# Two small remainders, one behind the other: an order on VectorE in each expert's second step

## The chip, the cores and the metric

One core of a Trainium2 chip runs the kernel. The metric is the device time of one execution in microseconds (us); the time before is the median of three runs. Lower is better.

## What is computed

One sequence of 256 positions, width 1024, in fp32, passes a first block and then a second one. The first block has two layers: attention with a gated convolution and a dense SwiGLU, then a spatial gate and a mixture of experts. The second has two layers of four kinds of attention with a squared-ReLU MLP. The change lies in the mixture of experts, of which the reference says:

```python
D_FF = 2816
N_EXPERTS = 8
TOP_K = 2

def moe_swiglu(h, router_w, w1, w3, w2):
    """Top-2-of-8 expert SwiGLU; tokens sorted by expert into padded blocks, only selected
    experts evaluated. h: (B,S,D); w1,w3: (E,D,F); w2: (E,F,D)."""
    ...
    def expert_block(args):
        xb, e = args
        return (jax.nn.silu(xb @ w1[e]) * (xb @ w3[e])) @ w2[e]
    ...
    contrib = y_sorted * gate_flat[order][:, None].astype(h.dtype)
    out = jax.ops.segment_sum(contrib, sorted_token, num_segments=n_tok)
```

## The kernel before

**Products in three parts.** Each operand of a large product is held as a high part `hi` in fp32r, a rounded form, and a remainder `lo` = value - `hi`. `product` (lines 519 to 521) issues three matmuls: hi x hi, then the two mixed ones. So each weight passes two engines before TensorE may use it. ScalarE copies a half slot (128 x 1024) from the ring into a buffer `w_hi` (line 2147), and VectorE subtracts it from the ring's value into `w_lo` (line 1312). The same is done to hidden features (`h_hi`, line 2410, and `h_lo`, line 1900) and to the outputs of an expert (`y_hi`, line 2416, and `y_lo`, line 1914).

**The stream of weights.** SyncE streams slots of 1 MB from HBM into a ring of six buffers (line 491). The refill of a buffer waits for `lo_ready` of both halves that it held, so for VectorE. The `w_hi`/`w_lo` buffers of the expert stage are four; the copy of half m waits until TensorE has done half m - 4. `reach(done)` says how many halves can be split once TensorE has done `done` of them, and `split_to(m)` splits all halves before m.

**The expert stage.** Eight experts of 11 steps each make 88 steps `s`, with `e = s // 11` and `j = s % 11`. A step takes three slots, six halves: four halves for the up products of 256 hidden features (w1 and w3 side by side), two for the down product of the step before. TensorE's order in a step is: two up halves, the transposes of the step before (`moe_turn`), two further up halves, the down product `moe_down(s - 1)`. The down product waits for `lo_ready` of its first half and for `moe.hidT_lo`, which `moe_lo(s - 1)` raises on VectorE; in the first down product of an expert also for `y_split`, since it starts to overwrite the banks from which `y_lo` is made.

**VectorE's order.** `moe_step` (lines 1918 to 1936) writes it out. It is `split_to`, `moe_lo(s - 1)` (the tile `h_lo`), `split_to` for two further halves, and the product of silu and gate (line 1929, written to a part of `arena`). In steps 2 and 3 of an expert the outputs of the expert before are merged (line 1906), one half of the tokens each. In the second step (j = 1) of experts 2 to 8 the remainder of the expert outputs is made too, by `split_y`: two instructions of 128 x 512. All engines run their queues in order, and a wait holds what stands behind it.

**ScalarE's order** in that second step is: `y_hi`, `w_hi` of both down halves, `h_hi`, then the next `w_hi`.

Of the kernel before, what the change touches and what calls it, by code (L numbers as in the profile page):

```python
# [108 lines left out]
def ada_before(n):  # L109

    q = PLACE["work", n]
    out = []
    while q and ORDER[q - 1][0] == "ada":
        q -= 1
        out.insert(0, ORDER[q][1])
    return out
# [16 lines left out]
def reach(done):  # L133

    m = done
    while m < 2 * SLOTS and BEFORE[m] < done:
        m += 1
    return m
# [5 lines left out]
def up_slot(s):  # L144

    return W_MOE + (3 * s - 1 if s else 0)
# [71 lines left out]
def build(nc, a, out):  # L218
# [3 lines left out]
    with ExitStack() as ctx:  # L222
# [101 lines left out]
        def half_buffer(m):  # L324
            b = BUFFER[m]
            return (w_hi[:, b, :], w_lo[:, b, :]) if b < PAIRS else (w_hi3[:, :], w_lo3[:, :])
# [944 lines left out]
        def _(dve):  # L1271
# [10 lines left out]
            def fold(slot):  # L1282

                l, q = slot // ADA_SLOTS, PLACE["ada", slot]
                dve.wait_ge(landed[q % RING], 16 * (q // RING + 1))
                for h in range(2):
                    i = 2 * (slot % ADA_SLOTS) + h
                    k, part = i // 6, i % 6
                    src = ring[:, q % RING, h * HALF:(h + 1) * HALF]
                    c = csilu[:, k:k + 1]  # L1290
                    if k == 0 and part < 4:
                        ins = dve.tensor_scalar(acc[:, part, :], src, c, None, ALU.mult)
                    else:
                        if k == 0:
                            dve.wait_ge(bada_in, 16 * (l + 1))
                        else:
                            dve.wait_ge(folded, 2 * ADA_SLOTS * l + i - 5)
                        ins = dve.scalar_tensor_tensor(out=acc[:, part, :], in0=src, scalar=c, in1=acc[:, part, :],  # L1298
                                                       op0=ALU.mult, op1=ALU.add)
                    ins.then_inc(folded, 1)  # L1300

            def split_to(m_end):

                for m in range(split_at[0], min(m_end, split_end[0])):
                    if m % 2 == 0:
                        for slot in ada_before(m // 2):
                            fold(slot)
                    dve.wait_ge(hi_ready, m + 1)
                    a = m % 2 * HALF
                    hi, lo = half_buffer(m)  # L1310
                    q = PLACE["work", m // 2]
                    dve.tensor_tensor(lo, ring[:, q % RING, a:a + HALF], hi.bitcast(F32), ALU.subtract)\  # L1312
                        .then_inc(lo_ready, 1)
                    split_at[0] = m + 1
# [562 lines left out]
            def select(w, n):  # L1877

                rank = col("slot", w.chunk * P, P)
                e = slice(n, n + 1) if isinstance(n, int) else bass.ds(n, 1)  # L1880
                for t in range(QB):
                    pl = place[:, t, e]
                    ins = dve.tensor_scalar(sel[:, t, :], rank, pl, None, ALU.is_equal)
                    if w is second_pass:
                        ins = dve.tensor_scalar(selg[:, t, :], rank, pl, gate[:, t, e], ALU.is_equal, ALU.mult)
                ins.then_inc(w.sel_ready, 1)

            def take(w, counts, c0=0):

                for h in range(2):  # L1890
                    dve.wait_ge(w.gathered_hi, counts[h])
                    f = slice(4 * h, 4 * h + 4)
                    dve.tensor_tensor(x_lo[:, f, c0:c0 + P], ps[:, 6 + h, :].rearrange("p (f c) -> p f c", f=4), x_hi[:, f, c0:c0 + P].bitcast(F32),
                                      ALU.subtract).then_inc(w.gathered_lo, 1)

            def moe_lo(s):

                dve.wait_ge(moe.hidT_hi, s + 1)
                c = 256 * (s % 2)
                dve.tensor_tensor(h_lo[:, s % 2, 0:256], ps[:, 2, c:c + 256], h_hi[:, s % 2, 0:256].bitcast(F32),  # L1900
                                  ALU.subtract).then_inc(moe.hidT_lo, 1)

            def moe_merge(e, t):

                dve.wait_ge(moe.scattered, 2 * e + t + 1)
                dve.scalar_tensor_tensor(out=resid[:, t, :], in0=bank(merge_bank(e, t), 2), scalar=gate[:, t, e:e + 1],  # L1906
                                         in1=resid[:, t, :], op0=ALU.mult, op1=ALU.add).then_inc(moe.merged, 1)

            def split_y(e):

                for h in range(2):
                    c = slice(h * BANK, (h + 1) * BANK)
                    dve.wait_ge(moe.y_kept, 2 * e + h + 1)
                    dve.tensor_tensor(y_lo[:, c], ps[:, 4 + h, :], y_hi[:, c].bitcast(F32), ALU.subtract)\
                        .then_inc(y_split, 1)

            def moe_step(s):

                e, j = s // J1, s % J1
                n = up_slot(s)  # L1920
                if s >= 1:
                    if j == 1 and e >= 1:
                        split_to(reach(2 * n + 1))
                        split_y(e - 1)
                    split_to(reach(2 * (n + 1)))
                    moe_lo(s - 1)
                split_to(reach(2 * (n + 2)))
                dve.wait_ge(moe.act_ready, s + 1)
                dve.tensor_tensor(hid_rows[:, s % 2, :], act_rows[:, s % 2, :], ps[:, s % 2, 256:512], ALU.mult)                    .then_inc(moe.hid_ready, 1)
                if e >= 1 and j in (2, 3):  # L1930
                    moe_merge(e - 1, j - 2)
                if j == 6 and e + 1 < NE:
                    dve.wait_ge(moe.selT_ready, e + 1)
                    select(moe, e + 1)
                if j == 8 and e + 1 < NE:
                    take(moe, [2 * e + 3, 2 * e + 4], P * ((e + 1) % 2))
# [52 lines left out]
            for s in range(STEPS):  # L1989
                moe_step(s)  # L1990
# [831 lines left out]
```

## Time and profile before

| | us |
|---|---|
| median of 3 runs | 2073.05 |
| lowest and highest of them | 2065.96, 2076.78 |
| the profiled execution | 2076.95 |
| its span, first to last instruction | 2074.8 |
| TensorE busy (PE) | 1970.3 |
| VectorE busy (DVE) | 1591.0 |
| ScalarE busy (ACT) | 1192.3 |

The profile is of one execution, which is not one of the three. Its busy times are shares of the span; what an engine waits for stands in the idle time ahead of an instruction. PE is TensorE's matmuls, PEld its weight loads, which overlap them. The expert stage lies between about 485 and 1287 us.

### The profile page before, as it was taken

To read this page: it belongs to the slowest core of one execution; us is meant where nothing else is said; L and a number is where in the kernel's file an instruction comes from. 1 tells how busy PE (TensorE), PEld (TensorE's weight loads), DVE (VectorE), ACT (ScalarE), POOL (GpSimd) and SP (SyncE) were. 2 spreads that over 40 slices of the span, in tenths; PEclk is the share of its full clock that TensorE was granted. 3 is DMA by queue.
4 is the path that set the end of the run, shared out by engine and by line. 5 is a ranking of instruction groups with operands and counts; after the bars stand their busy time and mean duration, and the time that the engine had idled before them with its cause. 6 is when DMAs were issued, how large, how long until landed. Compare 5 with 4: busy or idle time off the path is not lost.

```text
span 2074.8 us, 27900 instructions
## 1 busy us (share of the span) xinstructions
PE 1970.3 (95%) x11086; PEld 1694.4 (82%) x11086; DVE 1591.0 (77%) x1997; ACT 1192.3 (57%) x1638; POOL 29.8 (1%) x32
## 2 busy tenths in 40 slices
PE   7999999999999999999999998897999999899998
PEld 7889997877878787878787876797789988778997
DVE  5868886658898989898989897767479984746555
ACT  4444345337777777777777775556444445534443
POOL 0000000000000000000000000000000000000000
PEclk9999999999999999999999999899999999889999
DMA  7349885437888989898888887342168862304551
GB/s 298 138 143 348 330 331 188 173 112 296 340 340 342 344 339 343 338 341 342 339 342 338 343 343 293 122 142 102 61 234 344 337 257 107 122 28 166 183 188 56
DMA packets 71405, 512.02 MB, mean 247 GB/s; under 512 B 8162, under 2 KB 8546, under 8 KB 9826
## 3 DMA queue, kind: packets, MB, share of 16 engines
q1 hardware_dynamic: 69536, 504.40, 64.5%
q10 hardware_dynamic: 1732, 5.77, 0.8%
q8 instruction: 90, 1.47, 0.3%
q14 instruction: 47, 0.39, 0.1%
HBM read 509.08 MB, written 1.05 MB: 246 GB/s over the span
## 4 chain that ended last, share of the span: by engine, by line
PE 80%; DVE 12%; ACT 4%; issue 2%; POOL 1%; DMA 0%; POOLq 0%; ACTq 0%; SPq 0%; DVEq 0%
PE ps L519 24%; PE ps L521 23%; PE ps L520 23%; DVE w_lo L1312 6%; ACT w_hi L2147 2%; PE ps L732 1%; PE ps L945 1%; PE ps L528 1%; PE ps L684 1%; PE ps L698 1%; POOL stat L2592 1%; PE ps L963 1%; PE ps L790 1%; ACT score L2255 1%; DVE resid L1906 0%
## 5 line engine op out<-in xcount | busy, mean ns | idle before, releaser
L1312 DVE TENSOR_TENSOR w_lo<-ring,w_hi 128x1024 fp32r<-128x1024 f32 x862 | 1044.6, 1222 | 331.4 <-ACT w_hi L2147 304.0
L2147 ACT ACTIVATE w_hi<-ring 128x1024 fp32r<-128x1024 f32 x862 | 911.5, 1061 | 662.8 <-PE ps L521 655.9
L519 PE MATMUL ps<-w_hi,x_hi 128*128 128x512 f32 (+1 forms) x1056 | 408.5, 389 | 7.2 <-DVE x_lo L1600 3.3
L521 PE MATMUL ps<-w_hi,x_lo 128*128 128x512 f32 (+1 forms) x1056 | 400.4, 381 | 0.0
L520 PE MATMUL ps<-w_lo,x_hi 128*128 128x512 f32 (+1 forms) x1056 | 399.4, 380 | 0.0
L519 PE MATMUL ps<-x_hi,w_hi 128*128 128x256 f32 x1248 | 359.5, 288 | 5.0 <-DVE x_lo L1426 3.9
L520 PE MATMUL ps<-x_lo,w_hi 128*128 128x256 f32 x1248 | 355.1, 285 | 0.0
L521 PE MATMUL ps<-x_hi,w_lo 128*128 128x256 f32 x1248 | 354.8, 284 | 0.0
L519 PE MATMUL ps<-w_hi,h_hi 128*128 128x512 f32 x732 | 291.9, 399 | 18.7 <-DVE h_lo L1900 15.7
L520 PE MATMUL ps<-w_lo,h_hi 128*128 128x512 f32 x732 | 285.6, 390 | 0.0
L521 PE MATMUL ps<-w_hi,h_lo 128*128 128x512 f32 x732 | 285.1, 390 | 0.0
L519 PEld LDWEIGHTS ps<-x_hi,w_hi 128*128 128x128 f32 x1248 | 241.4, 193 | 10.6 <-issue 5.1
L520 PEld LDWEIGHTS ps<-x_lo,w_hi 128*128 128x128 f32 x1248 | 241.5, 194 | 1.7 <-issue 0.2
L521 PEld LDWEIGHTS ps<-x_hi,w_lo 128*128 128x128 f32 x1248 | 241.3, 193 | 0.0
L519 PEld LDWEIGHTS ps<-w_hi,x_hi 128*128 128x128 f32 (+1 forms) x1056 | 193.1, 183 | 48.1 <-DVE w_lo L1312 4.0
L521 PEld LDWEIGHTS ps<-w_hi,x_lo 128*128 128x128 f32 (+1 forms) x1056 | 192.7, 183 | 40.5
L520 PEld LDWEIGHTS ps<-w_lo,x_hi 128*128 128x128 f32 (+1 forms) x1056 | 193.3, 183 | 36.6
L519 PEld LDWEIGHTS ps<-w_hi,h_hi 128*128 128x128 f32 x732 | 137.7, 188 | 63.2 <-DVE h_lo L1900 34.4
L521 PEld LDWEIGHTS ps<-w_hi,h_lo 128*128 128x128 f32 x732 | 137.7, 188 | 29.6
L520 PEld LDWEIGHTS ps<-w_lo,h_hi 128*128 128x128 f32 x732 | 138.0, 188 | 25.0
L1298 DVE SCALAR_TENSOR_TENSOR arena<-ring,csilu,arena 128x1024 f32<-128x1024 f32 x88 | 108.9, 1278 | 0.0
L2255 ACT ACTIVATE score<-score,soft 128x128 f32<-128x128 f32 (+4 forms) x112 | 47.2, 424 | 34.7 <-DVE soft L1498 34.6
(269 smaller groups left out, 1459.0 us busy)
## 6 DMA issues: line engine op xcount, KB each, us to landing
ring<-in_stream SPq DMA_DIRECT2D x479, 1024.0 KB, 4.9
con<-in_consts ACTq DMA_DIRECT2D x1, 2048.0 KB, 21.7
arena<-in_ln_rows ACTq DMA_DIRECT2D x3, 512.0 KB, 3.9
resid<-in_x SPq DMA_DIRECT2D x1, 1024.0 KB, 6.6
arena<-in_fin_row ACTq DMA_DIRECT2D x2, 512.0 KB, 3.4
out<-rows SPq DMA_DIRECT2D x2, 512.0 KB, 2.6
arena<-in_w_s ACTq DMA_DIRECT2D x1, 512.0 KB, 5.9
con<-in_consts ACTq DMA_DIRECT2D x1, 237.0 KB, 4.3
```

What stands on the lines that cost most here:

```text
L519: pe.matmul(out_, lhs[0], rhs[0], start=start, stop=False)
L520: pe.matmul(out_, lhs[0], rhs[1], start=False, stop=False)
L521: return pe.matmul(out_, lhs[1], rhs[0], start=False, stop=stop)
L528: pe.matmul(ps[:, b, :], x_hi[:, 6, 0:P], x_lo[:, 4:6, :].rearrange("p a s -> p (a s)"), start=True, stop=True)
L684: last = pe.matmul(ps[:, b + u // 2, (u % 2) * S:(u % 2) * S + kw], q, k, start=True, stop=True)
L698: last = pe.transpose(ps[0:kp, 4 + n // 4, (n % 4) * P:(n % 4 + 1) * P], score[:, g % 2, u, kb * P:kb * P + kp], ident)
L732: last = pe.matmul(ps[:, mix_bank(layer, g), o * vw:(o + 1) * vw], probT[0:kp, g % 2, u * nkb + kb, :], v, start=kb == 0, stop=kb == nkb - 1)
L790: last = pe.matmul(ps[:, COLUMN_BANK[l][p0 // 2], c:c + 1], acc[:, part, f * P:(f + 1) * P], ones[:, 0:1], start=True, stop=True)
L1298: ins = dve.scalar_tensor_tensor(out=acc[:, part, :], in0=src, scalar=c, in1=acc[:, part, :], op0=ALU.mult, op1=ALU.add)
L1312: dve.tensor_tensor(lo, ring[:, q % RING, a:a + HALF], hi.bitcast(F32), ALU.subtract)\
L2147: act.activation(half_buffer(m)[0], ring[:, q % RING, a:a + HALF], ACT.Copy).then_inc(hi_ready, 1)
L2255: ins = act.activation(sc, sc, ACT.Exp, bias=soft[:, g % 4, 0, u:u + 1], scale=96.0 ** -0.5 if kind == "mla" else 0.125, accum_out=soft[:, ...
```

## The change

In the steps that make `y_lo` (j = 1 and e >= 1, seven of the 88), `moe_lo(s - 1)` is issued directly behind `split_y`, and the `split_to` that stood ahead of it comes after it. In the other steps the order is kept, in an `else` branch. Since `split_to(reach(2 * n + 1))` has already been issued in such a step, the `split_to` that is moved covers one half: the second half of the down slot.

```diff
                     if j == 1 and e >= 1:
                         split_to(reach(2 * n + 1))
                         split_y(e - 1)
-                    split_to(reach(2 * (n + 1)))
-                    moe_lo(s - 1)
+                        moe_lo(s - 1)
+                        split_to(reach(2 * (n + 1)))
+                    else:
+                        split_to(reach(2 * (n + 1)))
+                        moe_lo(s - 1)
                 split_to(reach(2 * (n + 2)))
```

VectorE's queue before, in the second step of the second expert, with what each instruction waits for:

```order
L1312 TENSOR_TENSOR w_lo<-ring,w_hi 128x1024 [waits hi_ready] x3
L1914 TENSOR_TENSOR y_lo<-ps,y_hi 128x512 [waits moe_y_kept] x2
L1312 TENSOR_TENSOR w_lo_51<-ring,w_hi_50 128x1024 [waits hi_ready]
L1900 TENSOR_TENSOR h_lo<-ps,h_hi 128x256 [waits moe_hidT_hi]
L1312 TENSOR_TENSOR w_lo<-ring,w_hi 128x1024 [waits hi_ready] x2
L1929 TENSOR_TENSOR arena<-arena,ps 128x256 [waits moe_act_ready]
```

The same place with the change (`w_lo_51` and `w_hi_50` are the fourth pair of weight buffers):

```order
L1312 TENSOR_TENSOR w_lo<-ring,w_hi 128x1024 [waits hi_ready] x3
L1914 TENSOR_TENSOR y_lo<-ps,y_hi 128x512 [waits moe_y_kept] x2
L1900 TENSOR_TENSOR h_lo<-ps,h_hi 128x256 [waits moe_hidT_hi]
L1312 TENSOR_TENSOR w_lo_51<-ring,w_hi_50 128x1024 [waits hi_ready]
L1312 TENSOR_TENSOR w_lo<-ring,w_hi 128x1024 [waits hi_ready] x2
L1932 TENSOR_TENSOR arena<-arena,ps 128x256 [waits moe_act_ready]
```

`h_lo` and the remainder of the down slot's second half have changed places; line 1929 is now called 1932.

TensorE's queue at the down product of the same step, which is the same in both kernels:

```order
L521 MATMUL ps<-w_hi,x_lo 128x512
L519 MATMUL ps<-w_hi,h_hi 128x512 [waits lo_ready,y_split,moe_hidT_lo]
L520 MATMUL ps<-w_lo,h_hi 128x512
L521 MATMUL ps<-w_hi,h_lo 128x512
L519 MATMUL ps<-w_hi,h_hi 128x512
L520 MATMUL ps<-w_lo,h_hi 128x512
L521 MATMUL ps<-w_hi,h_lo 128x512
L519 MATMUL ps<-w_hi_50,h_hi 128x512 [waits lo_ready]
```

Nothing moved here: the first of the six waits for `h_lo` and the first half's remainder, and the second half's remainder is asked for six matmuls later.

## Rows read from the trace of the kernel before

**Rows 1.** The page: busy time, granted TensorE clock in 40 slices, chain by engine.

```profile
PE 1970.3 (95%) x11086; PEld 1694.4 (82%) x11086; DVE 1591.0 (77%) x1997; ACT 1192.3 (57%) x1638; POOL 29.8 (1%) x32
...
PEclk9999999999999999999999999899999999889999
...
PE 80%; DVE 12%; ACT 4%; issue 2%; POOL 1%; DMA 0%; POOLq 0%; ACTq 0%; SPq 0%; DVEq 0%
```

**Rows 2.** Line 1900: who waited for `h_lo`, with us in all and times.

```profile
  PEld ps L519: 34.4, 59
  PE ps L519: 15.7, 22
```

**Rows 3.** TensorE in order of time: start, duration, instruction, idle time before it, releaser.

```profile
559.84 0.50 PE L519 MATMUL ps<-w_hi,h_hi 128*128 128x512 f32 x1 [0.31 <-DVE h_lo L1900]
...
587.02 0.50 PE L519 MATMUL ps<-w_hi,h_hi 128*128 128x512 f32 x1 [1.36 <-DVE h_lo L1900]
...
614.90 0.50 PE L519 MATMUL ps<-w_hi,h_hi 128*128 128x512 f32 x1 [0.43 <-DVE h_lo L1900]
...
688.87 0.50 PE L519 MATMUL ps<-w_hi,h_hi 128*128 128x512 f32 x1 [1.34 <-DVE h_lo L1900]
...
1198.37 0.50 PE L519 MATMUL ps<-w_hi,h_hi 128*128 128x512 f32 x1 [1.34 <-DVE h_lo L1900]
```

**Rows 4.** VectorE in order of time, steps 2 and 3 of the second expert.

```profile
583.08 1.22 DVE L1312 TENSOR_TENSOR w_lo<-ring,w_hi 128x1024 fp32r<-128x1024 f32 x1 [0.69 <-ACT w_hi L2147]
584.22 1.28 DVE L1914 TENSOR_TENSOR y_lo<-ps,y_hi 128x512 fp32r<-128x512 f32 x2
585.42 1.21 DVE L1312 TENSOR_TENSOR w_lo<-ring,w_hi 128x1024 fp32r<-128x1024 f32 x1
586.55 0.41 DVE L1900 TENSOR_TENSOR h_lo<-ps,h_hi 128x256 fp32r<-128x256 f32 x1
586.88 2.35 DVE L1312 TENSOR_TENSOR w_lo<-ring,w_hi 128x1024 fp32r<-128x1024 f32 x2
589.15 0.41 DVE L1929 TENSOR_TENSOR arena<-arena,ps 128x256 f32<-128x256 f32 x1
589.88 1.23 DVE L1312 TENSOR_TENSOR w_lo<-ring,w_hi 128x1024 fp32r<-128x1024 f32 x1 [0.32 <-ACT w_hi L2147]
591.26 3.95 DVE L1312 TENSOR_TENSOR w_lo<-ring,w_hi 128x1024 fp32r<-128x1024 f32 x3 [0.16 <-ACT w_hi L2147]
595.13 0.42 DVE L1900 TENSOR_TENSOR h_lo<-ps,h_hi 128x256 fp32r<-128x256 f32 x1
596.52 2.59 DVE L1312 TENSOR_TENSOR w_lo<-ring,w_hi 128x1024 fp32r<-128x1024 f32 x2 [0.98 <-ACT w_hi L2147]
599.03 0.41 DVE L1929 TENSOR_TENSOR arena<-arena,ps 128x256 f32<-128x256 f32 x1
599.36 1.28 DVE L1906 SCALAR_TENSOR_TENSOR resid<-ps,gate,resid 128x1024 f32<-128x1024 f32 x1
```

**Rows 5.** ScalarE in order of time, second step of the second expert.

```profile
583.88 0.38 ACT L2410 ACTIVATE h_hi<-ps 128x256 fp32r<-128x256 f32 x1
...
588.79 1.06 ACT L2147 ACTIVATE w_hi<-ring 128x1024 fp32r<-128x1024 f32 x1 [1.70 <-PE ps L521]
```

**Rows 6.** TensorE in order of time, its down product there and in the next step.

```profile
585.27 0.39 PE L521 MATMUL ps<-w_hi,x_lo 128*128 128x512 f32 x1
...
588.53 0.39 PE L519 MATMUL ps<-w_hi,h_hi 128*128 128x512 f32 x1
...
596.53 0.39 PE L519 MATMUL ps<-w_hi,h_hi 128*128 128x512 f32 x1
```

**Rows 7.** Line 491, us to landing; who kept ScalarE's line 2147 idle.

```profile
DMA to landing us min/median/max: 4.6/4.9/25.3
...
  DMA ring<-in_stream: 2.1, 1
```

**Rows 8.** Busy us by engine in stretches, then granted clock, DMA share, GB/s.

```profile
598.70:607.70 9.00, 9.00 (x43) 7.38 (x42) 8.51 (x10) 6.57 (x9) 0.00 (x0) 1.00 0.79 289
...
500.00:1280.00 780.00, 765.13 (x3520) 620.73 (x3519) 699.51 (x735) 597.01 (x715) 0.00 (x0) 1.00 0.90 342
1290.00:2074.00 784.00, 724.29 (x4628) 644.33 (x4627) 528.01 (x773) 366.36 (x609) 13.13 (x13) 0.95 0.44 162
```

## The prediction

> **What bounds the kernel now.** I read the page first: its busy shares, the granted clock by slice and the engine shares of the chain that ended last [rows 1]. TensorE is busy for 95% of the span and holds 80% of the chain, VectorE 12%. So a change on VectorE is worth only what TensorE waits for it. Next I read what waits for the feature remainder `h_lo` (line 1900): in the whole run TensorE's matmuls stood idle 15.7 us for it, in 22 waits [rows 2]. That is the ceiling of anything done for `h_lo`. Then TensorE's own order of time shows where those waits are [rows 3]. They repeat with each expert: about 1.35 us in the second step (j = 1), 0.43 us in the fifth (j = 4), about 0.3 us in the tenth (j = 9). The seven of the second step (experts 2 to 8; 1.36 once, 1.34 the other six times) make 1.36 + 6 x 1.34 = 9.4 us. The change touches these seven alone.
>
> Last I read VectorE, ScalarE and TensorE side by side around one of the seven, the second expert's at 587 us [rows 4, 5, 6]. TensorE has started its last up matmul at 585.27 (0.39 long, so done at 585.66) and needs `h_lo` for the down product. VectorE does meanwhile: weight remainder of the down slot's first half at 583.08, two `y_lo` from 584.22, weight remainder of the second half at 585.42, `h_lo` at 586.55. ScalarE's `h_hi`, from which `h_lo` is made, had been ready since 583.88 + 0.38 = 584.26. `h_lo` therefore waits for nothing but its place in VectorE's queue; it ends at 586.55 + 0.41 = 586.96, and TensorE starts at 587.02, 0.06 later.
>
> **The change, part by part.** Nothing is added or removed, no DMA is moved on its queue, and TensorE and ScalarE keep their orders. On VectorE, in seven places, `h_lo` changes places with one 128x1024 weight remainder.
>
> (a) *`h_lo` comes earlier.* VectorE's slot after the two `y_lo` opens at 585.42. There `h_lo` starts instead of at 586.55: 1.13 us earlier, one weight remainder from start to start (its own duration is 1.21, neighbours overlap by 0.08) [rows 4]. It ends at 585.42 + 0.41 = 585.83, and TensorE can start at 585.89 instead of 587.02. Its last matmul ended at 585.66, so it is still `h_lo` that is awaited, 0.23 us long. Gain: 1.13 us each, 7 x 1.13 = 7.9 us. The other six show the same wait to 0.02 us [rows 3], so I take them alike.
> The Trainium skill, Advanced Engine Details, section The Read-Write Bubble, says that the memory latency of VectorE lies open between instructions, the bus being pipelined within a tile but not between two. Taken strictly, the instruction moved away would be worth its whole 1.21 us and the seven 8.5 us; the rows with their overlap of 0.08 say 1.13, and the sum goes by the rows.
>
> (b) *The second half's remainder comes later.* It starts 0.33 us (586.88 - 586.55, the step from an `h_lo` to the next start) behind 585.42, at 585.75, and ends at 586.96 instead of 585.42 + 1.21 = 586.63. Who waits for it? TensorE's seventh matmul of the down product, which comes 588.53 - 587.02 = 1.51 us behind the first [rows 6]: now at 585.89 + 1.51 = 587.40. The remainder is there 0.44 us before. So it costs nothing; if the cover were gone, its price would be the part of its 1.21 us that sticks out. The refill of the ring's buffer also waits for this remainder and goes out 0.33 us later. SyncE's issues take 4.9 us (median) to land, in the whole run ScalarE waited once, 2.1 us, for a landing [rows 7], while a ring of six slots lies ahead. I cost it at nothing; as the rival on the refills it could be 7 x 0.33 = 2.3 us.
>
> (c) *The new wait.* `h_lo` waits for `h_hi`, and the second half's remainder, two more remainders and the product of line 1929 now stand behind that wait. `h_hi` is ready at 584.26, 1.16 us before 585.42 [rows 4, 5]: no cost. If it were later, the gain would fall one for one with what it is past 585.42, and be gone at 1.13 us.
>
> (d) *Is the gain kept?* From 586.88 on VectorE does the same work at the same times as before, while TensorE is 1.13 us ahead: VectorE is the one that is late. The test is whether it gets back its old distance before TensorE needs it. TensorE's down product of the first half ends earlier, so ScalarE's next weight copy, which waits for it, starts at 588.79 - 1.13 = 587.66 and is done at 588.72 [rows 5]. VectorE, after the line 1929 product at 589.15, is free for the next start at 589.15 + 0.33 = 589.48 (0.33 as from 599.03 to 599.36; before, it stood idle until 589.88). Four remainders at 1.13 each bring it to 594.0, and it then starts the `h_lo` of the next step, before at 595.13: 1.1 us earlier. The idle time before those four and inside them, 0.32, 0.16 and the gap inside the 3.95 us of three (3.95 against 1.21 + 2 x 1.13 = 3.47: 0.48), makes 0.96 and with the overlaps lost at each restart about 1.1 [rows 4]. Even if it lacked a tenth, 0.98 us of idle time stand directly behind that `h_lo` [rows 4], and TensorE wants that `h_lo` only at 596.53 - 1.13 = 595.40 [rows 6], with it done at 594.0 + 0.42 = 594.4. So by the end of the third step (j = 2) all three engines stand as before, 1.13 us earlier, and the waits of the fifth and tenth step stay at 0.43 and 0.3.
>
> **Sum.** 7 x 1.13 = 7.9 us off, with bounds of 7 x 1.13 - 2.3 = 5.6 (the refills of (b) on the path) and 9.4 (each of the seven waits gone). The profiled execution took 2076.95 us, 3.9 above the median of the three runs (2073.05); from it 2069.0, from the median 2073.05 - 7.9 = 2065.1. I give the one for the median. It is 0.38%. About 0.5% (10.4 us) is what a measurement of this kernel can tell from no change, and the three runs themselves lie 10.8 us apart, so I expect a true gain that counts as no change.
>
> **The rivals.**
> *The gain is taken back later (no change, 2073.0).* VectorE would be the bound of steps j = 2 to 4: it is busy for 8.51 of 9.00 us in one stretch there [rows 8], and it has a merge of 1.28 us in each of two steps. Then the wait of the fifth step would grow from 0.43 to 0.43 + 1.13 = 1.56. Against it stands the idle time of 0.98 us before 596.52, ended by ScalarE, which itself waits for TensorE: VectorE has caught up by then. It would decide only if the catching up of (d) fell short by over 2 us.
> *The refills become the path (slower, 2075.4).* The place is the ring buffer that is free only when the second half's remainder is done, 0.33 us later than before. The stage streams at a DMA share of 0.90 [rows 8], so there is little rate to spare; if ScalarE's copies waited for landings, each expert would lose the 0.33 and TensorE, waiting for weights, would have no use for the early `h_lo`: 2073.05 + 7 x 0.33 = 2075.4. It decides from the point at which a landing comes after ScalarE asks for it. One expert takes 688.87 - 587.02 = 101.85 us [rows 3] for 33 slots, 3.09 each; a buffer is wanted again about five slots after its refill goes out, 15 us, and the landing takes 4.9. So it is some 10 us from that point.
> *The clock falls elsewhere (about 2055 or 2075).* In the expert stage the granted clock is 1.00, i.e. 2.4 GHz, in spite of waits of 1.3 us; from 1290 us on it is 0.95 [rows 8], which is about a tenth of 784 us at the lower level, 78 us, costing half of them, 39. That stage gets the same work at other instants. A quarter more or less of it would be 10 us: 2065.1 - 10 = 2055, 2065.1 + 10 = 2075.
> The Trainium skill, TensorE: Matmul & The Clock Gate, Part 1, says that the instant at which the clock changes varies from run to run of one kernel. By that rule neither sign is favoured, and the 10.8 us between three runs of one kernel speak for it.
>
> **How the numbers follow.** Forecast (7.9 us off, waits of the second step down to 0.23): 0.74. Taken back later: 0.09. Refills on the path: 0.03. Clock elsewhere: 0.14, half of it each way. Predicted time: 2065.1. The forecast with its bounds and the uncertainty of a median of such runs (3 to 4 us) spans 2060 to 2070; the other cases are let in up to 2057.5 below and 2073.5 above, which takes in "taken back", leaves out both clock ends and the refills, and some of the scatter. Faster by over 0.5% needs 10.4 us: the scatter of the medians lifts 7.9 over it in about a fifth of the forecast's cases (0.15), plus the clock's good half (0.07): 0.22. Slower by over 0.5%: 0.02, the refills or the clock's bad half with scatter on top. Within 0.5%: the rest, 0.76.
>
> **What would show it.** In the profile after, TensorE's waits for `h_lo` fall from 15.7 to about 15.7 - 7.9 = 7.8 us, still 22 of them, the seven at 0.2 to 0.25. `h_lo` starts about 1.2 us behind the first `y_lo`, the second half's remainder 0.33 behind `h_lo`, and no wait for `w_lo` appears at the seventh down matmul. The distance between second steps of neighbouring experts (101.85 us) shrinks to 100.7. The fifth step's wait stays at 0.43. I am wrong if that one grows, if TensorE waits for line 1312, if ScalarE waits for landings in the expert stage, or if the expert stage is 8 us shorter and the rest after it longer.

## The result

| | before | with the change |
|---|---|---|
| median of 19 runs each, us | 2074.51 | 2063.65 |
| lowest and highest, us | 2065.96, 2080.97 | 2058.24, 2070.19 |
| profiled execution, us (span) | 2076.95 (2074.8) | 2059.92 (2057.8) |
| ratio, 95% interval | | 0.9943, 0.993 to 0.9955 |

The change makes the kernel faster by 0.57% by the ratio, with an interval of 0.45 to 0.70%. The medians lie 10.9 us (0.52%) apart, against the 7.9 us of the forecast. The profile after separates the two parts of this at once: the expert stage got shorter by nearly what was predicted, and the rest comes from elsewhere.

Line 1900 first, who waited for `h_lo`, in the kernel after (it answers [rows 2]):

```profile
  PEld ps L519: 26.5, 59
  PE ps L519: 7.8, 22
```

TensorE's matmuls wait 7.8 us where it was 15.7, in the same 22 places. TensorE in order of time, kernel after (start, duration, instruction, idle before it; it answers [rows 3, 6]):

```profile
585.30 0.39 PE L521 MATMUL ps<-w_hi,x_lo 128*128 128x512 f32 x1
585.89 0.50 PE L519 MATMUL ps<-w_hi,h_hi 128*128 128x512 f32 x1 [0.21 <-DVE h_lo L1900]
586.23 0.39 PE L520 MATMUL ps<-w_lo,h_hi 128*128 128x512 f32 x1
...
613.74 0.51 PE L519 MATMUL ps<-w_hi,h_hi 128*128 128x512 f32 x1 [0.44 <-DVE h_lo L1900]
...
686.62 0.50 PE L519 MATMUL ps<-w_hi,h_hi 128*128 128x512 f32 x1 [0.20 <-DVE h_lo L1900]
```

The wait of the second step has gone from 1.36 to 0.21 us, that of the fifth stays (0.44 against 0.43), and from one second step to the next it is 686.62 - 585.89 = 100.73 us instead of 101.85. VectorE in order of time, kernel after (it answers [rows 4]):

```profile
584.22 1.28 DVE L1914 TENSOR_TENSOR y_lo<-ps,y_hi 128x512 fp32r<-128x512 f32 x2
585.42 0.42 DVE L1900 TENSOR_TENSOR h_lo<-ps,h_hi 128x256 fp32r<-128x256 f32 x1
585.75 3.49 DVE L1312 TENSOR_TENSOR w_lo<-ring,w_hi 128x1024 fp32r<-128x1024 f32 x3
589.16 0.42 DVE L1932 TENSOR_TENSOR arena<-arena,ps 128x256 f32<-128x256 f32 x1
589.49 4.63 DVE L1312 TENSOR_TENSOR w_lo<-ring,w_hi 128x1024 fp32r<-128x1024 f32 x4
594.03 0.42 DVE L1900 TENSOR_TENSOR h_lo<-ps,h_hi 128x256 fp32r<-128x256 f32 x1
595.36 2.59 DVE L1312 TENSOR_TENSOR w_lo<-ring,w_hi 128x1024 fp32r<-128x1024 f32 x2 [0.92 <-ACT w_hi L2150]
```

`h_lo` starts at 585.42, the second half's remainder 0.33 behind it. From 589.49 VectorE does four remainders without a pause, where it had paused before each of the first two; by the next `h_lo` (594.03, before 595.13) it has caught up, and the pause behind it is 0.92 us (before 0.98). The length of the expert stage is taken from the start of its first transposes (line 963) to the start of the last expert's scatter (line 992). In the kernel before:

```profile
484.18 0.33 PE L963 MATMUL ps<-con,arena 128*128 128x128 f32 x1 [0.64 <-DVE arena L1929]
...
1287.07 0.74 PE L992 MATMUL ps<-y_hi,h_hi 128*128 128x512 f32 x1 [2.06 <-issue]
```

and after:

```profile
484.19 0.33 PE L963 MATMUL ps<-con,arena 128*128 128x128 f32 x1 [0.65 <-DVE arena L1932]
...
1279.33 0.47 PE L992 MATMUL ps<-y_hi,h_hi 128*128 128x512 f32 x1 [2.06 <-issue]
```

802.89 us have become 795.14: 7.75 less. The stage begins at the same time. What follows it took 2074.8 - 1287.07 = 787.7 us before and 2057.8 - 1279.33 = 778.5 after, 9.2 less, though none of its code was changed and TensorE has the same 4634 matmuls there in both traces. The same stretch of time by granted clock, before and then after (columns: busy us of PE, PEld, DVE, ACT, POOL, granted clock, DMA share, GB/s; it answers the last line of [rows 8]):

```profile
1290.00:2050.00 760.00, 708.56 (x4542) 630.84 (x4542) 513.75 (x756) 359.98 (x599) 11.65 (x11) 0.95 0.45 166
```

```profile
1290.00:2050.00 760.00, 715.45 (x4624) 637.67 (x4622) 519.64 (x757) 361.75 (x599) 10.58 (x10) 0.96 0.45 166
```

The work of after stands 7.75 us earlier in this stretch; in the 760 us TensorE issued 82 matmuls more, at a higher mean clock. This one pair of executions is an extreme one; how much of it stands in the medians is the second question of the experiments.

### The profile page after: what moved, and what is told of

The parts are those of the page before. It is cut to its first block, busy times and chain, and to the rows that moved or that the text cites. A ratio compares the mean times of both kernels' runs of the same rounds, so it can differ in the third digit from the quotient of the medians.

```text
span 2057.8 us, 27900 instructions
## 1 busy us (share of the span) xinstructions
PE 1962.3 (95%) x11086; PEld 1689.2 (82%) x11086; DVE 1589.1 (77%) x1997; ACT 1192.9 (58%) x1638; POOL 29.9 (1%) x32
## 4 chain that ended last, share of the span: by engine, by line
PE 80%; DVE 12%; ACT 4%; issue 2%; POOL 1%; DMA 0%; POOLq 0%; ACTq 0%; DVEq 0%
PE ps L519 24%; PE ps L521 23%; PE ps L520 23%; DVE w_lo L1312 6%; ACT w_hi L2150 2%; PE ps L945 1%; PE ps L732 1%; PE ps L528 1%; PE ps L684 1%; PE ps L698 1%; POOL stat L2595 1%; PE ps L963 1%; ACT score L2258 1%; PE ps L790 1%; PE ps L536 1%
## 5 line engine op out<-in xcount | busy, mean ns | idle before, releaser
L519 PE MATMUL ps<-w_hi,h_hi 128*128 128x512 f32 x732 | 292.5, 400 | 10.8 <-DVE h_lo L1900 7.8
```

The source lines that it names most:

```text
L519: pe.matmul(out_, lhs[0], rhs[0], start=start, stop=False)
```

## The experiments

Two questions were asked: whether the place of `h_lo` in the queue is the whole of the 7.75 us, and what the 3 us beyond are. "Stage" below is the expert stage as just measured, in each kernel's own profile, and "sum of waits" is what TensorE's matmuls stood idle for `h_lo`. A ratio is the time against that of the kernel before measured beside it, with its 95% interval. The edits show the lines that matter; where nothing else is said they are made in the kernel with the change.

### 1. One place further back

Against the kernel before, in the seven second steps alone:

```diff
                         split_y(e - 1)
-                    split_to(reach(2 * (n + 1)))
-                    moe_lo(s - 1)
+                        split_to(reach(2 * (n + 1)) + 1)
+                        moe_lo(s - 1)
```

> The opposite dose: in the seven second steps h_lo stands one weight remainder further back than before, behind the first half of the next slot too. Theory (h_lo's place in VectorE's queue is the whole wait, 1.13 us a place, and the seven experts are alike): TensorE's seven waits grow from 1.34 to about 2.47 us, its sum of waits for h_lo from 15.7 to 23.6, the expert stage is 7.9 us longer than before, the waits of the fifth step stay at 0.43. Rival (VectorE's load in steps j = 2 to 4 is the bound): part of the delay is absorbed or carried on, the fifth step's wait moves away from 0.43. For the whole time: 7.9 us slower than before (ratio 1.0038) if the extra gain of the change over 7.9 us was chance in the clock; more than that, about 12 (1.0057), if the shift itself moves the clock in a lasting way.

The sum of waits is 23.5 us, and the seven waits are 2.49 and six times 2.47. So the waits grew as expected. The stage, though, is 815.5 us, 12.6 more than before and not 7.9. The rest is the clock. TensorE in order of time in this kernel, second and fourth expert:

```profile
587.70 0.79 PE L519 MATMUL ps<-w_hi,h_hi 128*128 128x512 f32 x1 [2.49 <-DVE h_lo L1900]
588.29 0.63 PE L520 MATMUL ps<-w_lo,h_hi 128*128 128x512 f32 x1
588.72 0.63 PE L521 MATMUL ps<-w_hi,h_lo 128*128 128x512 f32 x1
...
796.70 0.50 PE L519 MATMUL ps<-w_hi,h_hi 128*128 128x512 f32 x1 [2.47 <-DVE h_lo L1900]
797.03 0.40 PE L520 MATMUL ps<-w_lo,h_hi 128*128 128x512 f32 x1
797.27 0.39 PE L521 MATMUL ps<-w_hi,h_lo 128*128 128x512 f32 x1
```

Behind one wait the matmuls take 0.63 us and follow one another by 0.43, behind an equal one 0.39 and 0.24. The busy time by stretch says why (clock is the third number from the right):

```profile
587.70:591.10 3.40, 3.40 (x8) 2.72 (x9) 1.41 (x2) 0.37 (x1) 0.00 (x0) 0.52 0.92 364
692.10:695.50 3.40, 3.37 (x10) 2.70 (x11) 1.72 (x3) 1.06 (x1) 0.00 (x0) 0.69 0.95 364
1002.90:1006.30 3.40, 3.37 (x10) 2.70 (x11) 1.57 (x3) 1.06 (x1) 0.00 (x0) 0.66 0.94 361
796.70:800.10 3.40, 3.40 (x15) 2.83 (x16) 1.97 (x3) 1.35 (x2) 0.00 (x0) 1.00 0.95 378
```

Behind three of the seven waits of 2.5 us the granted clock fell to the lower level, 1.2 GHz, for a while; in the first of these stretches 8 matmuls were started where the undisturbed one has 15, so about 7 x 0.23 = 1.6 us were lost. Three times that is 4.8, and 7.9 + 4.8 = 12.7. The distances from one second step to the next bear it out: 104.4 to 104.6 us behind the three waits with the lower clock, 103.0 to 103.3 behind the others. Why three of seven equal waits had it and four had not, no run shows. Waits of 1.36 us and less did this nowhere in the stage, in any of the profiles. The whole time is 2086.79 us, ratio 1.0047 (1.003 to 1.0063), compatible with both of the numbers expected.

### 2. Four of the seven places

```diff
-                    if j == 1 and e >= 1:
+                    if j == 1 and e % 2 == 1:
                         split_to(reach(2 * n + 1))
                         split_y(e - 1)
                         moe_lo(s - 1)
                         split_to(reach(2 * (n + 1)))
```

(With even `e`, experts 3, 5 and 7, the order of before is kept.)

> The change in four of the seven places only (experts 2, 4, 6, 8). Theory: four waits of 0.20 and three of 1.34, sum of waits for h_lo 15.7 - 4 x 1.13 = 11.2 us, expert stage 4.5 us shorter than before. Whole time 4.5 us shorter (ratio 0.9978) if nothing but the expert stage counts; a share of four sevenths of the measured 0.57% (0.9967) if each saved microsecond brings more than itself.

Sum of waits 11.0 us, stage 798.5 us, 4.4 shorter than before: the saving goes by the place, one by one. The whole time gives 0.9966 (0.9953 to 0.998), which holds both expectations and is nearer to the second. In both experiments the waits of the fifth step stayed at 0.43 to 0.44, so nothing is left of the idea that VectorE's load in the following steps takes part of the gain.

### 3. The remainder of the expert outputs first

```diff
                     if j == 1 and e >= 1:
-                        split_to(reach(2 * n + 1))
+                        split_to(reach(2 * n))
                         split_y(e - 1)
+                        split_to(reach(2 * n + 1))
                         moe_lo(s - 1)
```

> The change, and y_lo is put ahead of the remainder of the down slot's first half, into the 0.69 us in which VectorE stood idle there. Theory: y_lo from about 582.4, first half's remainder about 583.5 to 584.7, h_lo at about 584.6, done at 585.0 before TensorE's last up matmul ends at 585.66; the seven waits of 0.20 go to zero, 1.4 us less than with the change alone, sum of waits for h_lo 7.8 - 1.4 = 6.4 us. Rival: the first half's remainder now comes last and TensorE waits for it (line 1312) instead, or y_lo waits for y_hi and the remainders behind it come late, so that the stage gets longer.

VectorE in order of time in this kernel, then TensorE:

```profile
580.77 1.28 DVE L1914 TENSOR_TENSOR y_lo<-ps,y_hi 128x512 fp32r<-128x512 f32 x2
581.97 1.22 DVE L1312 TENSOR_TENSOR w_lo<-ring,w_hi 128x1024 fp32r<-128x1024 f32 x1
583.10 0.42 DVE L1900 TENSOR_TENSOR h_lo<-ps,h_hi 128x256 fp32r<-128x256 f32 x1
```

```profile
583.76 0.39 PE L521 MATMUL ps<-w_hi,x_lo 128*128 128x512 f32 x1
583.98 0.39 PE L519 MATMUL ps<-w_hi,h_hi 128*128 128x512 f32 x1
584.21 0.39 PE L520 MATMUL ps<-w_lo,h_hi 128*128 128x512 f32 x1
```

VectorE's pause of 0.69 us has been filled, and the down product follows the up product with no gap. The waits fell as expected, to 6.4 us in 15 places. The stage fell by more: 791.35 us, 3.8 less than with the change alone, not 1.4. The reason is in the rows. With a wait, however small, the last matmul before it is booked with its whole 0.39 us, though the next could start 0.23 after it (583.98 to 584.21); and the first matmul after a wait takes 0.50 instead of 0.39 and lets the second start after 0.34 (585.89 to 586.23 in the kernel with the change) instead of 0.23. So a wait that goes away whole gives back its length and 0.16 + 0.11 = 0.27 us: 7 x (0.20 + 0.27) = 3.3 of the 3.8; for the other 0.5 there is no account. Whole time: 2063.13 us, ratio 0.9942 (0.9928 to 0.9956).

### 4. The fifth and the tenth step too

```diff
+                    elif j == 9 or (j == 4 and e >= 1):
+                        split_to(reach(2 * n + 1))
+                        moe_lo(s - 1)
+                        split_to(reach(2 * (n + 1)))
                     else:
```

> The change, and h_lo stands ahead of the down slot's second half in the fifth step (j = 4, experts 2 to 8) and in the tenth (j = 9, all) as well. Theory: their waits of 0.44 and 0.34 go to zero, 7 x 0.44 + 7 x 0.34 = 5.5 us off the expert stage against the change alone, and of TensorE's 22 waits for h_lo in the matmuls the seven of 0.20 and the last one of 0.93 stay: sum about 2.4 us. Rival (VectorE's load is the bound there, since the steps before hold the merges and x_lo): the waits come back a step later or at line 1312, and the stage keeps its length.

The sum of waits is 2.4 us, as expected, with eight places left, and none of the rival's waits for weight remainders came up. The stage is 785.5 us, 9.6 less than with the change alone, where 5.5 were expected; 14 removed waits with 0.27 each are 3.8 more, 9.3 together. Whole time: 2053.47 us, ratio 0.99 (0.9885 to 0.9915).

### 5. The same swap where there is no wait

Here the seven second steps have the order of before, and `elif j in (3, 6, 8)` has the three lines of experiment 4.

> Control: the order of before in the seven second steps, and the same swap (h_lo ahead of the down slot's second half) in the fourth, seventh and ninth steps of all experts, 24 places in which TensorE does not wait for h_lo. Theory: the swap is worth only the wait that it shortens, so nothing: 22 waits and 15.7 us as before, expert stage 802.9 us, ratio 1.000. Rival: the swap in itself does something (VectorE's overlaps, earlier or later refills of the ring), 24 x 0.05 us or more, or a wait for line 1312 opens since the second half's remainder comes later.

The whole time says "nothing" (0.999, 0.9972 to 1.0007), but the stage is 801.6 us, 1.3 less than before, and that is no noise: the same stage repeats to 0.1 us elsewhere (795.14 and 795.04 in experiment 7). The expectation was wrong in that "no matmul waits" is not "nothing waits". Line 1900 in this kernel:

```profile
  PEld ps L519: 31.1, 42
  PE ps L519: 16.6, 22
```

The weight loads' waits for `h_lo` went from 59 to 42. Such a place in the kernel before, TensorE's matmuls and weight loads in order of time:

```profile
504.31 0.39 PE L521 MATMUL ps<-w_hi,x_lo 128*128 128x512 f32 x1
504.51 0.19 PEld L519 LDWEIGHTS ps<-w_hi,h_hi 128*128 128x128 f32 x1 [0.24 <-DVE h_lo L1900]
504.53 0.48 PE L519 MATMUL ps<-w_hi,h_hi 128*128 128x512 f32 x1
504.62 0.19 PEld L520 LDWEIGHTS ps<-w_lo,h_hi 128*128 128x128 f32 x1
504.85 0.39 PE L520 MATMUL ps<-w_lo,h_hi 128*128 128x512 f32 x1
```

No idle time stands before the matmul, but its weights were loaded only with it, and the next one starts 0.32 us later instead of 0.23. In the same place of the control kernel the load stands one matmul ahead:

```profile
502.78 0.39 PE L521 MATMUL ps<-w_hi,x_lo 128*128 128x512 f32 x1
502.78 0.19 PEld L519 LDWEIGHTS ps<-w_hi,h_hi 128*128 128x128 f32 x1
503.00 0.39 PE L519 MATMUL ps<-w_hi,h_hi 128*128 128x512 f32 x1
...
503.23 0.39 PE L520 MATMUL ps<-w_lo,h_hi 128*128 128x512 f32 x1
```

17 places at about 0.1 us are 1.7 us; the waits of the tenth step grew by 0.13 on the average, 0.9 us in all (15.7 to 16.6), presumably since a remainder now comes later in the step before. The balance, 0.8, is a part of the 1.3 measured, not all of it.

### 6. Where the other 3 us are

Each run comes with its span and its mean granted clock. The clock has two levels, 2.4 GHz (1.0) and 1.2 GHz (0.5), so time at the lower level is 2 x (1 - clock) x span. Within the runs of one kernel, 196 over all the kernels, the span goes up by 0.37 us for each us of it. The table takes that out:

| kernel | runs | mean span | mean clock | us at the lower level | span less 0.37 of it | against before | stage against before |
|---|---|---|---|---|---|---|---|
| before | 70 | 2072.6 | 0.9744 | 106.0 | 2033.3 | | |
| change | 19 | 2061.5 | 0.9765 | 97.0 | 2025.7 | -7.6 | -7.8 |
| 1, further back | 7 | 2082.3 | 0.9740 | 108.3 | 2042.3 | +9.0 | +12.6 |
| 2, four of seven | 8 | 2065.5 | 0.9759 | 99.7 | 2028.6 | -4.7 | -4.4 |
| 3, y_lo first | 6 | 2060.0 | 0.9748 | 103.7 | 2021.6 | -11.7 | -11.5 |
| 4, three steps | 5 | 2050.9 | 0.9768 | 95.2 | 2015.7 | -17.6 | -17.4 |
| 5, swap without wait | 11 | 2069.9 | 0.9752 | 102.8 | 2031.9 | -1.4 | -1.3 |

At an equal clock each of these kernels gains what its expert stage gains, to 0.2 us (experiment 1, whose stage has clock losses of its own, apart). For the kernels of experiments 7 to 9 the same reckoning gives -8.0 for the change once more (stage -7.9), -6.0, -4.5, -1.1 and +0.7 with 8, 15, 25 and 34 matmuls added (stage -6.1, -4.3, -2.0 and +0.1), +0.1 for experiment 8 (stage +0.3) and -22.2 for experiment 9 (stage -21.1); so it holds to about 1 us. What the change has beyond 7.8 us is a clock of 0.9765 against 0.9744: 9.0 us less at the lower level, 0.37 x 9.0 = 3.3 us.

The clock records in the two profiles say where that time is. Ahead of the stage both have 23.9 us at the lower level, inside it none; behind it the kernel before has 88.0 and the change 62.5. These 25.5 us less, at 0.37, are 9.4 us, and the part behind the stage was 9.2 us shorter. But the profile of the same changed kernel in experiment 7 has 70.1 us there, so a single pair of executions proves nothing about the means.

Two reasons for the better mean clock were tried: that the later stages run at other instants, and that idle TensorE in the seven places lowers the clock elsewhere.

### 7. The change once more, and its later stages moved back

The first run is the change itself, beside the two that follow it.

> The change as it stands, once more, on the chip and at the time of the two that follow. Its waits must be those of the profile after (seven of 0.20, sum 7.8 us, expert stage 7.75 us shorter). Both theories on the remaining 3 to 4 us start from here: if the whole time is again 11 to 12 us below before, with a mean granted clock about 0.002 higher, the extra is lasting; if it is 7 to 8 us and the clocks are alike, the extra was chance.

Measured: 2064.35 us, ratio 0.9944 (0.9923 to 0.9965), sum of waits 7.8, stage 795.0, clock 0.9762. The 11 us are there again.

Then 34 matmuls of no use were put in a place where nothing waits for them (`keep_warm(n, 3)` issues n matmuls of 512 columns whose result nobody reads):

```diff
+                if e == NE - 1 and j == 8:
+                    keep_warm(34, 3)
                 for h in range(2):
                     moe_up(2 * n + h, 2 * h, s, c0)
```

> The change, and 34 matmuls of no use in the ninth step of the last expert, 34 x 0.227 = 7.7 us, so that all that follows the expert stage stands at the instants of the kernel before. Position theory (the stages behind the experts get a better clock because they begin 8 us earlier): clock and whole time go back to those of before, ratio 1.000. Other theory (what is saved is saved where it stood, and the clock is either chance or hangs on the seven waits): the change plus 7.7 us, so ratio to before about 0.9943 + 0.0037 = 0.998, clock as with the change.

The stage is 803.0 us long, as before the change; the seven waits are at 0.20. The whole time is 2074.37 us, ratio 0.9999 (0.9986 to 1.0011), clock 0.9748. The 0.998 of the other theory lies outside. The 7.9 us of padding cost 10 us between the medians.

> The change and 8 matmuls of no use in the ninth step of the last expert, 1.8 us. Nothing but the 1.8 us: 2064.0 + 1.8 = 2065.8, ratio to before 0.9952. Position theory (34 of them brought 10.9 instead of 7.7 us): the extra 3 us come in part or whole, at 0.4 us a microsecond 2066.5, or all at once 2069.

> The same with 15 matmuls, 3.4 us. Nothing but that: 2067.4, ratio 0.9960. Position theory: 2068.8 if gradual (ratio 0.9967), up to 2070.6 if all at once; or the time of the change plus 3.4 with its clock of 0.9765 if only the place within one stretch of the clock counts.

> The same with 25 matmuls, 5.7 us. Nothing but that: 2069.7, ratio 0.9972. Position theory: 2072 (ratio 0.9983), clock near 0.975.

| matmuls added | stage longer by | whole time, ratio (interval) | clock | mean span longer by |
|---|---|---|---|---|
| 8 | 1.7 | 2068.81, 0.9965 (0.9948 to 0.9981) | 0.9755 | 3.3 |
| 15 | 3.5 | 2068.13, 0.9965 (0.995 to 0.9981) | 0.9760 | 4.0 |
| 25 | 5.7 | 2074.89, 1.0 (0.9982 to 1.0017) | 0.9744 | 9.9 |
| 34 | 7.9 | 2074.37, 0.9999 (0.9986 to 1.0011) | 0.9748 | 11.1 |

The waits are those of the change in all four. With 1.7 and 3.5 us the time moves by little more than is added; with 5.7 and 7.9 the whole extra gain is gone. For the 25 matmuls "nothing but that" (0.9972) lies outside the interval. Whether it comes back gradually or all at once can't be told from these four. Nor did any run add the 25 or 34 matmuls to the kernel before, so that they lower the clock by themselves, and not by moving what follows, is not ruled out.

### 8. The waits filled with matmuls of no use

```diff
+                if e >= 1 and j == 1:
+                    keep_warm(5, 3)
                 if s >= 1:
                     moe_down(s - 1)
```

(in the kernel before)

> The order of before, and five matmuls of no use ahead of the down product in each of the seven second steps, 1.14 us, inside the 1.34 us in which TensorE waits for h_lo. No time is saved there: h_lo comes when it came, the seven waits shrink to about 0.2 us in name only, and the expert stage keeps its 802.9 us. Waits theory (idle TensorE in the seven places lowers the granted clock elsewhere or later): the clock rises to that of the change and 3 to 4 us of the time go. Other theory: time and clock of before, ratio 1.000 within 0.1 to 0.2%.

The seven waits are 0.21, the stage is 803.2 us, and the whole time is 2072.88 us, ratio 0.9991 (0.9978 to 1.0004), clock 0.9756. The interval holds both theories, so this run doesn't separate them. Its clock is 0.0012 (95% interval 0.0001 to 0.0023) above that of before, with the later stages at nearly the same instants; so a part of the 3 us may hang on the idle times. Against its being the whole stands experiment 7, where all four kernels have the change's short waits and two of them have lost the extra gain.

### 9. Both additions

> Both additions together: y_lo ahead of the first half's remainder in the second step, and h_lo ahead of the second half's remainder in the fifth and tenth. Theory: only the last wait for h_lo (0.93 us, end of the last expert) stays. A wait that goes away whole gives back its length and 0.27 us more (the end of a matmul's 0.39 us counts as busy though the next could start after 0.23, and the first one after a wait takes 0.11 longer): against the version with three steps 7 x (0.20 + 0.27) = 3.3 us off the expert stage, 785.5 - 3.3 = 782.2 us; whole time 20 to 24 us below before (ratio 0.990 to 0.988). Rival: the two additions share VectorE's idle time and one of them does not pay.

```diff
                     if j == 1 and e >= 1:
-                        split_to(reach(2 * n + 1))
+                        split_to(reach(2 * n))
                         split_y(e - 1)
+                        split_to(reach(2 * n + 1))
                         moe_lo(s - 1)
                         split_to(reach(2 * (n + 1)))
+                    elif j == 9 or (j == 4 and e >= 1):
+                        split_to(reach(2 * n + 1))
+                        moe_lo(s - 1)
+                        split_to(reach(2 * (n + 1)))
```

Line 1900 in this kernel:

```profile
  PEld ps L519: 10.4, 37
  PE ps L519: 0.9, 1
```

One wait in the matmuls is left. The stage is 781.8 us (expected 782.2), 21.1 less than before. Four runs have a median of 2049.46 us, ratio 0.9869 (0.9844 to 0.9893). This version beats both kernels. With the rule of 0.27 us a wait, learnt from experiments 3 and 4, the sum was right to half a us.

## Why the prediction came out as it did

**(a), the price of one place.** Right: `h_lo` at 585.42 and TensorE at 585.89, both to the hundredth, the seven waits at 0.20 to 0.21 where 0.2 to 0.25 were expected, the stage 7.75 us shorter against 7.9. Experiments 1 and 2 give the same price in the waits, with the opposite sign and in part. Here both ends of the comparison were waits that did not vanish; only so did the idle time shown give the saving. Two general statements ahead of (a) are wrong. The 15.7 us of waits are not "the ceiling of anything done for `h_lo`": experiment 9 took away 14.8 us of them and shortened the stage by 21.1, and experiment 3, with all seven waits gone, by 11.5, more than the bound of 9.4. And a change on VectorE is not worth "only what TensorE waits for it": experiment 5 gave 1.3 us with no less idle time in the matmuls, in part since weight loads were held up less. VectorE's instructions kept their start-to-start times, so the overlap of 0.08 us was rightly taken off. By the reading of the Trainium skill, Advanced Engine Details, section The Read-Write Bubble, at its strictest, a place is worth 1.21 us and the seven 8.5; the trace has `h_lo` 586.55 - 585.42 = 1.13 us earlier, so the measurement decides against it.

**(b), the second half's remainder.** Costed at nothing, and nothing came: it ran from 585.75, and in the whole run TensorE's matmuls waited 1.2 us for line 1312, where it was 1.8. The refills, 0.33 us later, were the rival with the price of 2.3 us; ScalarE still waited for a landing only once, 2.3 us (before 2.1), and the stage is no longer for it.

**(c), the new wait**, cost nothing. `h_hi` stood ready at 584.27, 1.15 us ahead of `h_lo`'s start.

**(d), whether VectorE catches up.** Right. The start times 589.48 and 594.0 and the wait of 0.43 in the fifth step were predicted; 589.49, 594.03 and 0.44 were measured. The rival "taken back later" falls with it.

**The sum is where the prediction was off**: 7.9 us against 10.9 between the medians. The measured time lies in the range, 1.5 us below the time forecast. That it is so near is in part luck: the median of three runs from which I started was 1.5 us below that of 19, which made up for half of the missing 3 us. The change came out at 0.52 to 0.57%, just beyond the 0.5% that I had taken as the border, to which I had given a chance of 0.22; the interval reaches down to 0.45%. The step that was off is the rival on the clock. It had the right place (all that stands behind 1290 us, at 0.95), and perhaps the right cause (the same work at other instants), but I took it as a coin with two equal sides, out of the sum. The runs show a difference that repeats: in 19 and again in 6 runs the change had 0.0018 to 0.0021 more of the clock (all 25 together 0.0020, 95% interval 0.0009 to 0.0030), worth 3 us, and in the kernel with 34 matmuls, which put the later stages back to their old instants, it was gone. I also charged half a us for each us at the lower level, where the runs show 0.37: the 78 us cost about 29 and not 39. The sign of the difference could not have been had from the trace of the kernel before. Its size could in part: the three runs, 10.8 us apart, and the 78 us at the lower level say that a few us of clock must be counted beside any saving of this size. The Trainium skill, TensorE: Matmul & The Clock Gate, Part 1, was read too broadly. It says that the instant of a change of clock varies from run to run of one kernel. That agrees with the traces: of two profiled executions of the changed kernel, one has a clock of 1.00 in its first 100 us, the other 0.98. That the means of two kernels should then be equal was my step, not the page's, and the runs contradict it.

**What stays open.** Why the mean clock of the changed kernel is better. That the later stages begin 7.8 us earlier is the likeliest reason by experiment 7, but it is not a rule of the kind "earlier is better". In experiment 3 they begin 11.5 us earlier and the clock is 0.9748, hardly that of before, in 4 and 9 17.4 and 21.1 us earlier with 0.9768 and 0.9760, and in 8 at the old instants with 0.9756. Each of these means, of 4 to 12 runs, is uncertain by 0.001 to 0.003. The steps of experiment 7 are too coarse for a law, and the profile is of one run of each kernel.

## What to carry to other kernels

Where a consumer waits for a small result that stands ready-to-make behind larger work in another engine's queue, moving it ahead is worth the number of places times the start-to-start distance there, as long as a wait is left, and that can be taken from one timeline; check only that what is put behind has a consumer that comes late enough. A wait that is shortened gives back what is shown, one that is removed gives back about 0.27 us more here, so the last 0.2 us of a wait are worth 0.47 or a little more. Ask for the mean clock of every run before a difference of a few tenths of a per cent is explained by the code: at an equal clock the kernels here agreed with their own traces to about 1 us (experiment 1 aside, which lost clock in the stage itself), without it they were off by up to 4 (experiment 4: mean span 21.7 us shorter, stage 17.4).

## What the runs showed of the hardware that was not expected

- Idle time before a matmul understates the wait. The matmul before it counts 0.39 us as busy where 0.23 would do, and the first one after it delays its successor by 0.11.
- A weight load that waited 0.24 us (504.51) cost 0.1 us though no matmul shows any idle time.
- With TensorE otherwise busy throughout, waits of up to 1.36 us never lowered the granted clock in the expert stage, and behind waits of 2.47 to 2.49 us it fell in three cases of seven, each costing about 1.6 us more.
- The mean granted clock differs between kernels whose later stages are the same code: 0.9765 and 0.9762 for the change, 0.9744 and 0.9748 with 25 and 34 matmuls added ahead of those stages. The span follows with 0.37 us for each us at the lower level. What sets the difference is not shown.
